# Order of work at five hand-overs of a two-block transformer kernel on one core

## The reference

```python
# first block, depth 1
h = h + concat([attention, mlstm, gating]) @ w_out
xt = rms_norm(h, norm2_g)
g_top = argmax(xt @ rg_w + rg_b)                       # 4 groups of 8 experts
e_val, e_loc = top_k(logits of the group, 2)
e_w = softmax(e_val) * softmax(group logits)[g_top]    # the tokens' weights
h = h + sum over the two experts of e_w * (silu(xt @ w_gate[e]) * (xt @ w_up[e])) @ w_down[e]
h = h + sigmoid(rms_norm(h) @ ple_gate_w) * (p @ ple_proj_w)
x = rms_norm(h, final_g)
# second block, two layers; layer 0 mixes by a short convolution, layer 1 by attention
b, c, v = split(rmsnorm(x) @ sc_w_in, 3)
x = x + (b * causal_conv3(c * v)) @ sc_w_out
g, u = split(causal_conv3(rmsnorm(x) @ ffn_w_up), 2)
x = x + (silu(g) * u) @ ffn_w_down                     # 2816 hidden columns, both layers
```

## Time and profile before

| | |
|---|---|
| median of three runs | 1121.35 us |
| profiled execution, time | 1122.01 us |
| its span | 1120.1 us |
| TensorE busy | 1067.8 us (95%) |
| VectorE busy | 868.3 us (78%) |
| ScalarE busy | 713.7 us (64%) |
| GpSimd busy | 136.8 us (12%) |
| mean granted TensorE clock | 0.988 |
| read from memory | 230.85 MB |

### The profile page before, as it was taken

How to read it: one execution, slowest core, us unless ns; L and a number is a source line. 1 busy time by engine, 2 the same in 40 slices (tenths; PEclk the granted TensorE clock), 3 DMA queues, 4 the chain that set the end, 5 groups by cost and what they waited for, 6 DMA issues and landing times.

```text
span 1120.1 us, 17261 instructions
## 1 busy us (share of the span) xinstructions
PE 1067.8 (95%) x6370; PEld 925.7 (83%) x6370; DVE 868.3 (78%) x1116; ACT 713.7 (64%) x946; POOL 136.8 (12%) x88
## 2 busy tenths in 40 slices
PE   7999978999999999999999999999999999999997
PEld 5877867777877877778989999999778879999996
DVE  5498678998989899877656776776777867877776
ACT  6677477888888888765434554454557765644543
POOL 1001100000000000012000232331200000423310
PEclk9999989999999999999999999999999999999999
DMA  9440617888888888854554445545443244556431
GB/s 372 169 156 32 215 54 284 321 339 329 333 317 336 335 335 338 301 188 155 184 189 140 185 171 218 189 158 183 182 151 104 85 151 156 207 183 217 163 145 37
DMA packets 33603, 232.61 MB, mean 208 GB/s; under 512 B 3856, under 2 KB 3984, under 8 KB 6032
## 3 DMA queue, kind: packets, MB, share of 16 engines
q1 hardware_dynamic: 32688, 229.98, 55.5%
q10 hardware_dynamic: 864, 1.93, 0.5%
HBM read 230.85 MB, written 1.05 MB: 207 GB/s over the span
## 4 chain that ended last, share of the span: by engine, by line
PE 74%; DVE 13%; ACT 6%; issue 4%; POOL 2%; DMA 1%; DVEq 0%; ACTq 0%; SPq 0%; POOLq 0%
PE bank L1944 10%; PE bank L1946 10%; PE bank L1945 10%; PE bank L2454 8%; PE bank L2455 8%; PE bank L2456 8%; PE bank L2309 5%; PE bank L2310 4%; DVE wlo L1147 4%; PE bank L2292 2%; ACT whi L524 1%; PE bank L2317 1%; PE bank L2357 1%; PE bank L2358 1%; DVE arena L1703 1%
## 5 line engine op out<-in xcount | busy, mean ns | idle before, releaser
L1147 DVE TENSOR_TENSOR wlo<-raw,whi 128x2048 fp32r<-128x2048 f32 x212 | 481.9, 2287 | 66.9 <-ACT whi L524 65.8
L524 ACT ACTIVATE whi<-raw 128x2048 fp32r<-128x2048 f32 x213 | 405.4, 1913 | 83.3 <-PE bank L1946 50.2
L2454 PE MATMUL bank<-xs,whi 128*128 128x256 f32 x896 | 251.2, 280 | 1.5 <-DVE wlo L1147 1.5
L2455 PE MATMUL bank<-xs,whi 128*128 128x256 f32 x896 | 250.2, 279 | 0.0
L2456 PE MATMUL bank<-xs,wlo 128*128 128x256 f32 x896 | 250.0, 279 | 0.0
L2454 PEld LDWEIGHTS bank<-xs,whi 128*128 128x128 f32 x896 | 168.4, 188 | 3.5 <-DVE wlo L1147 2.1
L2455 PEld LDWEIGHTS bank<-xs,whi 128*128 128x128 f32 x896 | 168.4, 188 | 0.9
L2456 PEld LDWEIGHTS bank<-xs,wlo 128*128 128x128 f32 x896 | 168.4, 188 | 0.0
L1944 PE MATMUL bank<-whi,rounded 128*128 128x512 f32 x344 | 139.3, 405 | 13.6 <-DVE rounded L1546 8.7
L1945 PE MATMUL bank<-wlo,rounded 128*128 128x512 f32 x344 | 136.7, 397 | 0.0
L1946 PE MATMUL bank<-whi,rounded 128*128 128x512 f32 x344 | 136.6, 397 | 0.0
(11 more groups left out here) (331 smaller groups left out, 1563.3 us busy)
## 6 DMA issues: line engine op xcount, KB each, us to landing
raw<-stream SPq DMA_DIRECT2D x215, 1024.0 KB, 4.8
arena<-finals ACTq DMA_DIRECT2D x3, 512.0 KB, 5.6
xres<-x_in SPq DMA_DIRECT2D x2, 512.0 KB, 4.8
raw<-stream SPq DMA_DIRECT2D x4, 256.0 KB, 6.1
out<-xn SPq DMA_DIRECT2D x4, 256.0 KB, 2.1
par<-params SPq DMA_DIRECT2D x1, 844.0 KB, 12.2
cst<-table SPq DMA_DIRECT2D x1, 502.0 KB, 8.8
arena<-p_in ACTq DMA_DIRECT2D x1, 256.0 KB, 5.9
```

The costliest lines, as they stand in the source:

```text
L524: act.activation(whi[:, s, :], raw[:, a, :], ACT.Copy).then_inc(S("high_done"), 1)
L1147: dve.tensor_tensor(wlo[:, s, :], raw[:, unit0 % RAW, :], whi[:, s, :].bitcast(F32), ALU.subtract)\
L2454: pe.matmul(o, whi[:, s, w], xhi[:, kk, :], start=first, stop=False, skip_group_check=True)
L2455: pe.matmul(o, whi[:, s, w], xlo[:, kk, :], start=False, stop=False, skip_group_check=True)
```

## The change

It reorders work and moves two waits; no operation is added or taken away.

1. Tokens' weights: `token_weights` is dissolved. Its first part stands ahead of VectorE's first gather copy, the second between its first and second. In pair 0 VectorE does `ahead(4)` before `hidden`, and the first rest before the second fold. ScalarE does the first Silu before the second gate-up copy, the first rounding before the second gather copy, and the third gather copy before `ahead(5)`.
2. ScalarE and VectorE split unit U_SCIN + 2 earlier: ScalarE between the squares of the first half and the copies of the turned second half, VectorE directly behind its part of those.
3. TensorE makes the roots' row ahead of step 4 of the second group instead of step 1.
4. Two of the four rests of the short convolution are made ahead of the last group's products; TensorE waits for the fifth group only before the output product's first chunk, and for the sixth before its second.
5. Dense blocks: the split of unit u0 + 4 moves ahead of the first expert's taps on both engines; in the last expert VectorE's split of unit u0 + 32 moves behind the first product and second root.

```diff
@@ pair_act, x.p0 == 0
                     out(0)
                     ahead(4)
+                    silu_pair(x, 0)
                     gate_up_out(x, 1)
+                    hidden_high(x, 0)
                     out(1)
-                    silu_pair(x, 0)
+                    out(2)
                     ahead(5)
+                    silu_pair(x, 1)
+                    back_out(x)
+                    out(3)
+                    hidden_high(x, 1)
+                    return
@@ scalar block
             squares_both(1, 0, 2)
+            split_to(U_SCIN + 2)
             turn_act(4, range(4, KD))
...
                 act.activation(root_row, bank[4][:, 0:T], ACT.Copy).then_inc(S("root_ready"), 1)
+                split_to(u0 + 4)
                 ffn_act(layer, 0, None, 0)
@@ vector block
             dve.tensor_reduce(V("spill"), V("over"), AX.X, ALU.add).then_inc(S("routed"), 1)
+
+            dve.wait_ge(S("router_exp"), 1)
+            gw, p1, p2 = V("gw"), V("p1"), V("p2")
+            link(dve.tensor_reduce(gw, eg, AX.X, ALU.add))
+            dve.wait_ge(S("router_exp"), 2)
+            link(dve.scalar_tensor_tensor(p1, dv, 1.0, gw, ALU.add, ALU.mult))
+            link(dve.reciprocal(p1, p1))
+            link(dve.tensor_tensor(p2, p1, dv, ALU.mult))
             gather_out(1, 0, 2)
             dve.wait_ge(S("ranked"), 2)
             dve.tensor_copy(spill_count[:], bank[0][0:1, 256:257]).then_inc(S("spill_known"), 1)
+            dve.tensor_tensor(oh1, oh1, over(p1, NE), ALU.mult)
+            link(dve.tensor_tensor(oh2, oh2, over(p2, NE), ALU.mult))
+            dve.tensor_tensor(oh1, oh1, oh2, ALU.add).then_inc(S("wt_ready"), 1)
+            dve.wait_ge(S("wt_ready"), 1)
+            link(dve.tensor_copy(wsp[:, 0], two(V("oh1"))))
+            link(dve.tensor_tensor(wsp[:, 1], two(V("oh1")), wsp[:, 0].bitcast(F32), ALU.subtract))
+            quad_weights(slice(0, 4), 0, S("wt_ready"))
+            quad_weights(slice(4, 8), 1, S("wt_ready"))
             gather_out(4, 1, 2)
...
                 fold(x, 0)
+                ahead(4)
+                hidden(x, 0)
                 if x.p0 == 0:
-                    token_weights()
-                    hidden(x, 0)
-                    ahead(4)
+                    hidden_low(x, 0)
+                    fold(x, 1)
                 else:
-                    ahead(4)
-                    hidden(x, 0)
-                fold(x, 1)
-                hidden_low(x, 0)
+                    fold(x, 1)
+                    hidden_low(x, 0)
                 hidden(x, 1)
...
             turn_dve(4, range(4, KD))
+            split_to(U_SCIN + 2)
...
                 split_to(U_SCIN + 2 * i + 3)
                 g = G_SC + i
+                if i == 5:
+
+                    sc_low(0)
+                    sc_low(1)
...
-            for f in range(4):
-                dve.wait_ge(S("sc_high"), f + 1)
-                dve.tensor_tensor(xlo[:, 2 * f:2 * f + 2, :], scy[:, 2 * f:2 * f + 2, :],
-                                  xhi[:, 2 * f:2 * f + 2, :].bitcast(F32), ALU.subtract).then_inc(S("sc_ready"), 1)
+            sc_low(2)
+            sc_low(3)
@@ ffn_dve
                 ins.then_inc(S("rooted"), 1)
+                if e0 == 0:
+                    ahead(5)
                 dve.wait_ge(S("rooted"), d0 + 1 + e)
@@ ffn_last_dve
                 tap(0)
-                split_to(u0 + 3 * FE - 1)
                 product(0)
                 root(1)
+                split_to(u0 + 3 * FE - 1)
                 rest(0)
@@ tensor block
-            group(G_SC + 1, U_SCIN + 2, ahead_of={1: lambda: row_of(both, bank[6], 5)})
+            group(G_SC + 1, U_SCIN + 2, ahead_of={4: lambda: row_of(both, bank[6], 5)})
...
+            pe.wait_ge(S("g_free"), G_SC + 5)
+            dense(C_SCOUT, U_SCOUT, "sc_ready")
             pe.wait_ge(S("g_free"), G_SC + 6)
-            dense(C_SCOUT, U_SCOUT, "sc_ready")
             dense(C_SCOUT + 1, U_SCOUT + 2, None, True, lambda: [turn_tile(5, t, range(4)) for t in range(TT)])
```

More of the change, by code:

```diff
@@ L1514, in _ @@
             split_to(U_MOE + 3)
[L1516 to L1533, removed]
             def fold(x, e):
@@ L1630, in _, with sc_low @@
             turn_dve(4, range(4, KD))
+            split_to(U_SCIN + 2)
+            def sc_low(f):
+                dve.wait_ge(S("sc_high"), f + 1)
+                dve.tensor_tensor(xlo[:, 2 * f:2 * f + 2, :], scy[:, 2 * f:2 * f + 2, :],
+                                  xhi[:, 2 * f:2 * f + 2, :].bitcast(F32), ALU.subtract).then_inc(S("sc_ready"), 1)
             for i in range(6):
```

## The result

The changed kernel takes 1110.59 us (median of four runs, 1110.04 to 1111.41) against 1122.03 for the kernel before (four runs, 1119.44 to 1123.87): a ratio of 0.989, 95% interval 0.9873 to 0.9907, or 11.4 us. The forecast was 1109.7, with a range of 1105.5 to 1114.5. The profiled execution took 1110.44 us with a span of 1108.6, 11.5 less than the span before.

The account below looks back on a forecast made before the run. TensorE's own work plus its stops, and the slow clock behind long ones, was taken to bound the kernel. Gains of 3.1 + 1.35 + 3.95 + 1.85 + 1.4 = 11.7 us off the 1121.35 median gave 1109.7, range 1105.5 to 1114.5.

Parts of the forecast that it names:

- Pair 0: Pair 0's down products: 3.83 us stop plus 1.6 of slow clock shrink to 2.3 in all; gain 3.1 us.
- copies late, clock falls: Lower end for pair 0: gather copies come late and the clock falls; gain only 1.0 us.
- Entry: Short convolution's second group: stops of 0.72, 0.93, 0.42 go, one of 1.6 comes at the third; net 1.35 us.
- The convolution's end: Ahead of the short convolution's output product: 2.27 us of stop and 1.7 of slow clock go; gain 3.95 us.
- First experts: First expert of each dense block: the 1.28 us stop goes, about 0.35 comes back later; gain 0.92 each.
- Last experts: Last expert of both dense blocks: 1.4 us gained in the first, 0 to 0.1 in the second; together 1.4.
- The one wait for the stream: Expert pairs of the kernel before: a single 1.7 us wait for a transfer; more than one afterwards would be wrong.
- the slower rival: Expert pairs: the 1.7 us wait for a transfer comes in each of 14 pairs; 1133.5 us, chance 0.02.
- (a) to (d): Forecast 0.55, slower clock 0.20, pair 0 gaining only 1.0 0.09, left-over stops not arising 0.07; together 0.91.
- (d): Left-over stops in the edited places don't arise, 2.0 + 1.6 + 0.7 more gained; 1105.4 us, chance 0.07.
- The rival of the slower clock: Short convolution's third group: row's later place makes a 1.6 us stop that slows the clock; 1111.4 to 1113.1, chance 0.20.

Follow-up runs that it names:

- ScalarE's half: Kernel before with only ScalarE's new order in pair 0, the vector block left as it was: 1119.07 us, ratio 0.996.
- VectorE's half: Kernel before with only VectorE's new order in pair 0, including the moved tokens' weights, the scalar block left as it was: 1121.51 us, one run.
- unit earlier alone: Kernel before with unit U_SCIN + 2 split earlier on both engines, the roots' row left at step 1: 1124.39 us, one run.
- pair 0 alone: Kernel before with only change 1, tokens' weights amid the gathers and both engines' new order in pair 0: 1119.22 us, ratio 0.9974.
- convolution's end alone: Kernel before with only change 4, the short convolution's rests and TensorE's moved wait: 1119.01 us, ratio 0.9961.
- splits ahead of taps: Changed kernel with both engines' split of the fifth unit moved ahead of the taps in every expert: 1109.89 us, ratio 0.9881.

## Why the prediction was right

- **Pair 0, 3.1.** Measured 3.1 in the changed kernel and 2.9 to 3.2 in the five other kernels that have the whole edit (M1 to M2 32.30 to 32.47 against 35.35 to 35.46). The stops forecast were 1.4, 0.5 and 0.4; they are 1.04, 0.31 and 0.33, each a little less, at the places and with the releasers named: the fourth gather's copy (176.50 against 176.6), unit 5's rest (178.47 against 178.3), unit 6 (181.86 against 181.5). The forecast counted them from the time at which TensorE is free; counted so, with 0.16 added, they are 1.2, 0.5 and 0.5, 0.1 less in all than the 2.3 forecast. The bounds for the gather's copy, 176.3 and 177.1, don't quite follow from the durations given, which make 176.3 without the copy's own 0.60 and 176.9 with it; ScalarE's instructions overlapped six times, by 0.10 to 0.14, and the copy ended at 176.45. What the step had wrong is its weight between the two halves: it opened with the tokens' weights and counted them as half of the case, and ScalarE's half alone gives everything. The bound of 1.0, "copies late, clock falls", is what VectorE's half alone gives, for the other reason.
- **Entry, 1.35.** Measured 1.1; the new stop was forecast at 1.6 and is 1.59. The step that the two edits are one was argued; the runs now show that neither gains it apart: -1.1 (with a slow clock) and 0.14. Missing from the working was GpSimd: its first small instruction, which is done twice, ran into the splits that VectorE now does there (last section) and took 1.7 us more each time. rstd_f was in time because GpSimd had been held up about as long in the kernel before, at two other instructions. That cancelling was luck: the working had not looked at it.
- **The convolution's end, 3.95.** Measured 3.7 in the changed kernel, and alone 3.2, or about 3.8 with the slower pace taken out. The step took for granted that the stop of 2.07 brings a slow stretch of 1.7. It is worth 1.5 of time when it comes (from that product to M4 216.64 us in the kernel before, 215.11 with the unit earlier alone, where the clock held), and it comes in six of eight traces. In the profiled execution of the kernel before it had come; where it doesn't, this edit gains about 2.2.
- **First experts, 2 x 0.92.** 0.90 and 0.87, with 0.35 and 0.36 coming back where the step said.
- **Last experts, 1.4.** 1.6 and 0.2. The term is too small by 0.4: I left 0.2 of the stop standing because ends are modelled long, and the view's 1.44 is 1.6 from start to start. The same holds for the second block, where the 0.09 in the timeline is 0.25.
- **The one wait for the stream** The earlier trace rows is absent from the changed kernel's pairs, so the slower rival had nothing to stand on there. The three waits in the run of VectorE's half, 2.5 us, are the nearest thing to it.

The sum, 11.7, met 11.5 between the spans and 11.4 between the medians. Part of that is cancelling: the entry and the convolution's end gave 0.25 less each, the last experts 0.4 more. The agreement of the medians has luck in it too, since each execution has a slow-clock part that no edit controls: nine runs of pair 0 alone form two heaps, five at 1118.5 to 1119.2 and four at 1121.3 to 1121.7. The profiled one of 1121.72 had the stretch at 92 us, and that of ScalarE's half, 1119.13, had not; their M1 differ by 2.4. That the other heap runs differ by the same thing is likely and not shown, for they have no trace.

The range was said to take in (a) to (d), but (d) at 1105.4 lies 0.1 below its lower end; nothing hangs on that here.

**The rival of the slower clock** had 0.20 and rested on 1.59 lying close to 1.44. In all traces together, these are the stops of 1.44 us and more at the edited places, and whether the granted clock fell to half behind them:

| stop | where | clock fell |
|---|---|---|
| 3.83 | pair 0 | 6 of 6 |
| 3.08, 2.98 | pair 0; third group | 2 of 2 |
| 2.07 | convolution's end | 6 of 8 |
| 1.58, 1.59 | third group | 0 of 3 |
| 1.50, with 0.42 behind it | row at step 1 | 1 of 1 |
| 1.44 to 1.51 | last expert | 0 of 8 |

So the length alone doesn't decide: 1.50 was followed by a slow stretch once and 2.07 twice was not. "1.44 didn't, 2.07 did", read from one trace, was a weaker argument than it looked, and the chance of 0.20 was not too large. The Trainium skill (TensorE: Matmul & The Clock Gate, Part 1) says that the number of slow products after a start differs from run to run of one kernel. These traces agree that it differs: ahead of M1, in code that is the same in all kernels, 1.71 us of clock were lost in one trace, 3.41 in seven and 5.12 in six. What decides it was not tested.

## What to carry to other kernels

When an engine stops for a chain that two engines share, work out the chain for each half of the reordering: here one engine's order gave all of the gain, and two edits elsewhere were worth 1.1 us only together. The arithmetic that shows a stop gone also shows where the next one comes; if that can be moved by whole steps (the row), price the neighbouring steps too, for one step earlier was 1.4 us better and one step later 2.9 worse. Of the 20 stops of 1.50 to 3.83 us in the table above, 15 had a slow stretch behind them, which cost about 1.5 more where it could be compared; count it as a chance and not as a rule. And look at what VectorE's large instructions hold up on GpSimd, before and after a move.

## What the runs showed of the hardware

**What a slow stretch costs.** Behind a single stop the loss was 1.70 or 1.71 us of clock in every trace where there was one, and around the gathers 3.41 or 5.12. In time it is a little less: behind pair 0's stop in the kernel before, products of 512 columns begin every 0.43 us from 178.90 to 181.46 instead of every 0.23, and eight of them lose 1.6 us. Windows over the gathers, before and after:

```profile
152.00:162.00 10.00, 7.37 (x35) 7.00 (x36) 6.46 (x18) 4.64 (x10) 0.00 (x0) 0.52 0.17 54
```

```profile
152.00:162.00 10.00, 6.61 (x36) 6.04 (x36) 8.53 (x30) 5.69 (x11) 0.00 (x0) 0.66 0.15 54
```

**The clock also fell where TensorE didn't stop.** The same window ahead of all edits, in the kernel before and in the changed one with the row at step 3; TensorE's timeline has no stop but one of 0.22 us between 60 and 98 us in either:

```profile
92.00:97.00 5.00, 5.00 (x26) 3.80 (x25) 2.85 (x10) 4.96 (x5) 0.59 (x1) 1.00 0.00 0
```

```profile
92.00:97.00 5.00, 5.00 (x16) 3.71 (x15) 2.08 (x6) 4.94 (x5) 1.26 (x1) 0.66 0.00 0
```

Six of the fourteen traces have this stretch, and all of those reach M1 1.4 to 2.5 us later than the other eight. Why it comes in some executions is open.

**A small GpSimd instruction waits for VectorE's split.** GpSimd and VectorE in the changed kernel, then GpSimd in the kernel before:

```profile
508.10 2.01 POOL L1097 TENSOR_SCALAR total<-sumsq 128x1 f32<-128x1 f32 x1 [22.92 <-ACT arena L871]
```

```profile
507.66 2.28 DVE L1156 TENSOR_TENSOR wlo<-raw,whi 128x2048 fp32r<-128x2048 f32 x1
```

```profile
511.20 0.30 POOL L1088 TENSOR_SCALAR total<-sumsq 128x1 f32<-128x1 f32 x1 [22.91 <-ACT arena L864]
```

The same instruction takes 0.30 us, and 2.01 when it starts inside the split; it ends 0.17 behind the split's end. The Trainium skill (SBUF — State Buffer, "Who interferes with whom") states that an instruction of VectorE with two inputs in SBUF contends with one of GpSimd that reads SBUF, and that the ports the two engines share are an exclusive lock. The traces agree; the split reads two tiles.

The kernel before had the same thing at another place, and there it made the row late. GpSimd, then VectorE:

```profile
514.44 1.99 POOL L1095 TENSOR_TENSOR both<-rstd 128x1 f32<-128x1 f32 x1
516.39 2.60 POOL L1096 TENSOR_TENSOR rstd_f<-total,cst 128x1 f32<-128x1 f32 x1
```

```profile
514.08 4.49 DVE L1147 TENSOR_TENSOR wlo<-raw,whi 128x2048 fp32r<-128x2048 f32 x2 [3.24 <-ACT whi L524]
```

In the changed kernel these two instructions take 0.19 and 0.55. So the hold-up was 1.80 + 2.05 = 3.85 us before and is 1.71 + 1.65 = 3.36 after, at other instructions, and rstd_f is complete 12.66 us behind M3 before and 12.18 after. The row's stops of 0.93 and 0.42 are gone because the row moved, not because GpSimd was quicker. An estimate from these rows: with neither hold-up rstd_f would have been there at about 516.0 in the kernel before, ahead of the row at step 1, for which TensorE was ready at about 518. That placement of the splits was not run. For a move of VectorE's large splits this means that GpSimd's small instructions have to be placed too.

**The pace of 256-column products has two values.** In some executions these products begin every 116.7 ns, in others every 117.8, all through the convolution's groups and at a granted clock of 1.00. The changed kernel, and the same with the row at step 3:

```profile
533.79 0.28 PE L2471 MATMUL bank<-xs,whi 128*128 128x256 f32 x1
...
565.99 0.28 PE L2471 MATMUL bank<-xs,whi 128*128 128x256 f32 x1
```

```profile
533.80 0.28 PE L2470 MATMUL bank<-xs,whi 128*128 128x256 f32 x1
...
565.95 0.28 PE L2470 MATMUL bank<-xs,whi 128*128 128x256 f32 x1
```

There are 276 products from the first of these rows to the last in the one and 273 in the other, in 32.2 us each. Five of the fourteen traces have the slower pace (pair 0 alone, convolution's end alone, unit earlier alone, row at step 3, splits ahead of taps); over the groups behind M3 it is 0.5 us. What sets it is open.
